# One block from the projection on, an early second feed product, and turnings moved in the output product

## The reference, cut to what matters

```python
n = _rms_norm(x, norm_attn_g)
q, k, v of both mixers = n @ w_in                      # 3072 columns
mixed = concat(diff_attention(...), stick_breaking(...))  # 512 + 512 columns
h = x + mixed @ w_out
n2 = _rms_norm(h, norm_ffn_g)
y = h + (silu(n2 @ w_gate) * (n2 @ w_up)) @ w_down      # D_FF = 2816
y = _rms_norm(y, norm_final_g)
```

## Time and profile before

| What | Value |
|---|---|
| median of 3 runs | 1412.73 us (1412.57 to 1413.26) |
| the profiled execution, its own time | 1409.75 us |
| its span in the profile | 1407.9 us |
| busy, PE | 1361.4 us, 97% of the span |
| busy, DVE | 999.7 us, 71% |
| busy, ACT | 623.8 us, 44% |
| busy, POOL | 450.8 us, 32% |
| mean granted clock | 0.993 |

### The profile page before, as it was taken

The page is one execution under the profiler, slowest core; times in us unless marked ns, Lnnn a source line. Parts: engine busy times, 40 slices in busy tenths (PEclk is TensorE's granted clock), DMA queues, the critical chain, the costliest instruction groups (busy, mean ns, idle before and its releaser), DMA issues. The chain is left out here.

```text
span 1407.9 us, 23796 instructions
## 1 busy us (share of the span) xinstructions
PE 1361.4 (97%) x9152; PEld 1193.8 (85%) x9152; DVE 999.7 (71%) x1317; ACT 623.8 (44%) x1112; POOL 450.8 (32%) x416
## 2 busy tenths in 40 slices
PE   6999999989999999999789999999999999999997
PEld 5778888768888777788689999999999998787886
DVE  5896858688868999756687766566766566754466
ACT  6634333288887887333352122222132233533343
POOL 2133341200010000111174454454454454644353
PEclk9999999999999999999999999999999999999999
DMA  7265542464444544433234543444443448855554
GB/s 254 72 213 192 204 154 73 146 181 138 126 127 121 148 136 135 156 127 96 65 121 144 174 137 123 150 145 145 174 143 116 150 163 290 303 175 164 164 180 172
DMA packets 172200, 218.05 MB, mean 155 GB/s; under 512 B 19836, under 2 KB 110328, under 8 KB 170680
## 3 DMA queue, kind: packets, MB, share of 16 engines
q1 hardware_dynamic: 163416, 193.13, 42.3%
q0 software_dynamic: 3840, 12.58, 2.7%
q10 hardware_dynamic: 4832, 10.82, 2.1%
HBM read 152.98 MB, written 63.50 MB: 154 GB/s over the span
## 5 line engine op out<-in xcount | busy, mean ns | idle before, releaser
L792 PE MATMUL ps_proj<-shared 128*128 128x512 f32 x224 | 90.1, 402 | 2.7 <-DVE shared L546 1.8
L2663 ACT COPY aux<-ps_feed 128x544 f32<-128x544 f32 x22 | 13.5, 612 | 170.3 <-PE ps_feed L2984 170.3
L793 PE MATMUL ps_proj<-shared 128*128 128x512 f32 x224 | 88.1, 393 | 0.0
L794 PE MATMUL ps_proj<-shared 128*128 128x512 f32 x224 | 88.1, 393 | 0.0
L2613 POOL TENSOR_TENSOR ring_more<-staging,ring_more 128x512 fp32r<-128x512 f32 x45 | 69.5, 1550 | 56.5 <-ACT ring_more L2649 56.4
L2613 POOL TENSOR_TENSOR shared<-staging,shared 128x512 fp32r<-128x512 f32 x41 | 60.0, 1467 | 86.1 <-ACT shared L2649 86.1
L1431 ACT COPY aT<-ps_aT 128x512 f32<-128x512 f32 (+2 forms) x168 | 81.1, 526 | 9.8 <-PE ps_aT L1760 9.0
L1760 PE MATMUL ps_aT<-ident,z 128*128 128x128 f32 (+1 forms) x568 | 83.3, 280 | 1.9 <-DVE z L1603 1.7
L2877 DVE TENSOR_TENSOR blocks<-ps_feed,blocks 128x512 f32<-128x512 f32 x56 | 36.0, 682 | 66.4 <-PE ps_feed L3013 66.4
L1603 DVE TENSOR_TENSOR_SCAN z<-z,near 128x1024 f32<-128x1024 f32 (+7 forms) x64 | 81.5, 1336 | 0.0
L2982 PE MATMUL ps_feed<-shared,ring_more 128*128 128x272 f32 x264 | 76.6, 290 | 2.4 <-issue 2.4
(11 more groups left out here) (372 smaller groups left out, 4520.5 us busy)
## 6 DMA issues: line engine op xcount, KB each, us to landing
staging<-s_dram SPq DMA_DIRECT2D x50, 256.0 KB, 4.2
staging<-in_w_gate SPq DMA_DIRECT2D x11, 1024.0 KB, 7.8
blocks<-in_w_up SPq DMA_DIRECT2D x11, 1024.0 KB, 5.3
blocks<-in_w_down SPq DMA_DIRECT2D x11, 1024.0 KB, 9.8
t_dram<-blocks SPq DMA_DIRECT2D x11, 1024.0 KB, 3.9
s_dram<-blocks SPq DMA_DIRECT2D x11, 1024.0 KB, 5.2
w_raw<-in_w_in SPq DMA_DIRECT2D x10, 1024.0 KB, 6.6
staging<-in_cache_sb_v POOLq DMA_DIRECT2D x31, 256.0 KB, 3.1
```

Source lines behind the costliest of these rows:

```text
L792: nc.tensor.matmul(res, a_hi[:, k, cols], b_hi[:, k], start=start, stop=False)
L793: nc.tensor.matmul(res, a_hi[:, k, cols], b_lo[:, k], start=False, stop=False)
L794: return nc.tensor.matmul(res, a_lo[:, k, cols], b_hi[:, k], start=False, stop=(k == HK - 1))
L2663: nc.scalar.copy(two(first), bank(u, 0)).then_inc(first_done, 1)
```

## The change

It has four parts.

1. **One block.** `feed` uses `t["block"]`, and `border.close()` comes after it, so no engine waits at the end of mix.
2. **Product 1 of unit 0 early.** `early_product_pe` makes product 0 and then product 1 behind tile 8's matmuls, ahead of `turn_n(8)`; the second waits for the sums of tile 7. Weight block 1 is split into mT_lo in place of `shared`, by ACT right behind block 0 and by POOL right behind block 0; POOL now first waits for the normed rows of tile 7. Feed's PE loop starts at product 2.
3. **Left columns of product 2 (the third) without the sample.** For c = 0 it waits for `n_lo` of the first three chunks only. ACT splits weight block 2 ahead of the last columns of part 2, and waits for two products ahead of the split of part 6.
4. **Turnings.** `turn_m(1)` goes ahead of the last 24 matmuls of tile 0, and `turn_m(2)` behind the left half of tile 1, ahead of `turn_n(0)`.

```diff
 mix:
-        t["ring_first"][0] = [mT_hi[:, late, a * HK:(a + 1) * HK] for a in range(2)]
+        t["ring_first"] = [[x[:, late, a * HK:(a + 1) * HK] for a in range(2)] for x in (mT_hi, mT_lo)]
...
@ gpsimd
-                if i >= NT - 1:
-                    w_low_pool(nc, pool, t, i - NT + 1)
+                if i == NT - 1:
+                    pool.wait_ge(normed, NT - 1)
+                    w_low_pool(nc, pool, t, 0)
+                    w_low_pool(nc, pool, t, 1)
...
@ scalar
-                if i == NT:
-
-                    act.wait_ge(mixed, 2 * NT)
-                    w_high_act(nc, act, t, 1)
...
                         w_high_act(nc, act, t, 0)
+                        w_high_act(nc, act, t, 1)
...
@ tensor
             turn_m(0)
             multiply_first(1, range(HK, KD))
+            turn_m(1)
             pe.wait_ge(m_lo, 2)
             multiply_first(0, range(HK)).then_inc(mixed, 1)
-            turn_m(1)
             multiply_first(1, range(HK)).then_inc(mixed, 1)
             pe.wait_ge(*t["outputs_made"])
             for i in range(1, NT):
-                if i + 1 < NT:
+                if 2 < i + 1 < NT:
                     turn_m(i + 1)
...
+                    if j == 0 and i == 1:
+                        turn_m(2)
                     if j == 0:
                         turn_n(i - 1)
             pe.wait_ge(m_lo, 2 * NT)
-            first_product_pe(nc, pe, t, 3 * NC - 2)
+            early_product_pe(nc, pe, t, 0, 3 * NC - 2)
+            pe.wait_ge(h_added, 2 * (NT - 1))
+            early_product_pe(nc, pe, t, 1, 3 * NC - 1)
             turn_n(NT - 1)
...
 early_product_pe(nc, pe, t, m, parts_done), in place of first_product_pe:
-    pe.wait_ge(t["w_lo_done"], 1)
+    pe.wait_ge(t["w_lo_done"], m + 1)
     pe.wait_ge(t["n_lo"], parts_done)
-    w_hi, w_lo = t["ring_first"][0]
+    w_hi, w_lo = t["ring_first"][m]
-        res = t["ps"][:, 0, c, 0:CW]
+        res = t["ps"][:, m, c, 0:CW]
-            x_hi, x_lo = t["part_hi"][0][:, k, cols], t["part_lo"][0][:, k, cols]
+            x_hi, x_lo = t["part_hi"][m][:, k, cols], t["part_lo"][m][:, k, cols]
...
 feed:
-        block = ctx.enter_context(nc.Block(no_gpsimd_drain=True))
+        block = t["block"]
...
@ scalar
+            split_w(2)
             split_n(2)
-            split_w(2)
             split_n(3)
             split_w(3)
...
                 if u == 0 and s in (0, 1, 2):
+                    if s == 2:
+                        act.wait_ge(multiplied, 2)
                     split_n(4 + s)
...
@ tensor
-                if u == 0:
-                    pe.wait_ge(n_lo, parts_done(s))
                 pe.wait_ge(w_lo_done, m + 1)
                 w_hi, w_lo = ring[m % RING]
                 for c in range(2):
+                    if u == 0 and s == 2 and c == 0:
+                        pe.wait_ge(n_lo, 3 * (NT // 2 - 1))
+                    elif u == 0:
+                        pe.wait_ge(n_lo, parts_done(s))
...
-                for s in range(0 if u else 1, NPROD):
+                for s in range(0 if u else 2, NPROD):
                     product(u, s)
...
 encoder_step:
             mix(nc, t)
-            border.close()
             feed(nc, t)
+            border.close()
```

More of the change, by code:

```diff
@@ L2225, in w_low_pool, with early_product_pe @@
     nc.gpsimd.tensor_tensor(w_lo, first_blocks(t)[m], w_hi.bitcast(F32), ALU.subtract).then_inc(t["w_lo_done"], 1)
-def first_product_pe(nc, pe, t, parts_done):
-    pe.wait_ge(t["w_lo_done"], 1)
+def early_product_pe(nc, pe, t, m, parts_done):
+    pe.wait_ge(t["w_lo_done"], m + 1)
     pe.wait_ge(t["n_lo"], parts_done)
-    w_hi, w_lo = t["ring_first"][0]
+    w_hi, w_lo = t["ring_first"][m]
     HK, CW = w_hi.shape[1], t["half"] // 2
@@ L3163, in encoder_step @@
                                 .rearrange("p (k n) -> p k n", k=HK) for a in range(2))
-            at = 6 * WIDTH + 2 * HK * P
-            t["ring_first"] = [None, [shared[:, at + a * HK * P:at + (a + 1) * HK * P]
-                                      .rearrange("p (k n) -> p k n", k=HK) for a in range(2)]]
             mix(nc, t)
+            feed(nc, t)
             border.close()
-            feed(nc, t)
 _INS = ['x_prompt', 'x_sample', 'cache_diff_k', 'cache_diff_v', 'cache_sb_k', 'cache_sb_v', 'norm_attn_g', 'w_in',
```

## The result

The changed kernel took 1414.88 us, median of 22 runs (1412.96 to 1417.08), against 1412.74 us for the kernel before over 22 runs beside it (1410.71 to 1415.44). The ratio is 1.0018, with a 95% interval of 1.0012 to 1.0023: some 2.5 us slower (2.1 us by the medians), clear of zero, and by the bound of 0.2% still no change that a single measurement could tell. The profiled execution took 1416.36 us (span 1414.4 us), one of the longer ones.

A forecast was written before the change was run, and what follows sets the result against it. PE was taken to bound the start, DVE's chain the seam. Terms +1.5 + 0.05 + 0.16 = +1.7 us gave 1411.4 us for the profiled execution, 1414.4 us for the median; range 1410.6 to 1418.2 us.

The forecast's parts named there:

- The hole behind turning 2: Start of output product: PE waits 4.2 us for tile 0's normalised rows, whose turning starts 1.5 us later.
- Turning 1 costs nothing: Turning 1, ahead of tile 0's last 24 matmuls, finds its input ready; costed at nothing, some tenths if that cover went.
- Tile 7's normalisation: At the seam, L2039 runs without POOL's collision, so tile 7's row turning on PE gains 1.02 us.
- Two POOL instructions delay DVE by 2 x 1.2 us: POOL's two weight-split instructions move onto five DVE additions behind tile 7's normalisation and delay them, 2.4 us in all.
- First early product: PE's first early product, waiting for DVE's first L2047, starts at 690.2 instead of 689.52 us.
- Turning 8 and the block's end: At the seam, turning 8 with ACT's copies comes +0.05 us later; the long split that starts DVE's chain, +0.16 us.
- the encounter of POOL with L2732: POOL's L2613 (1.3 us) meets the DVE step the prediction calls L2731, which ends at 701.75 instead of 701.10 us.
- Products 2 and 3 early: At the seam, 4.4 us leave PE and the third product finishes some 3 us sooner; neither is waited for, no gain.
- the bound at the seam: DVE's chain, not PE, sets the seam; the rival that PE sets it had chance 0.07 and gave 1408.8 us.
- The clock: Rival, chance 0.38: granted clock falls in the new hole behind turning 2, costing 3 us, 1417.4 us.
- main case: Start and seam terms summed, no added clock fall: 1414.4 us, own range 1412.0 to 1415.5 us, chance 0.45.

The follow-up runs named there:

- x6: c with tile 0's square, normalisation and additions moved ahead of work waiting on turning 2 or tile 2's heads, turnings kept; 1407.94 us, ratio 0.9976 to the kernel before.
- x2: c with 16 added matmuls of 512 columns, read by nothing, in PE's hole behind turning 2; 1412.33 us, ratio 1.0001 to the kernel before.
- c: The changed kernel itself, with all four parts of the change; 1414.88 us, ratio 1.0018 to the kernel before.
- x1: c with turning 2 back at the head of tile 1's product, turning 1 still early; 1412.62 us, ratio 1.0003 to the kernel before.
- x3: c without POOL's wait for tile 7's normalised rows; 1415.72 us, ratio 1.0022 to the kernel before.
- x8: The kernel before with one block in place of two and nothing else; 1412.67 us, ratio 1.0003 to the kernel before.
- x4: c with the second early product behind the last turning instead of ahead of it; 1415.43 us, ratio 1.0023 to the kernel before.
- x12: c with the third product waiting for all its columns ahead of the left ones; 1415.75 us, ratio 1.0023 to the kernel before.
- x9: x6 with DVE's two weight sums moved out from ahead of the first two parts' low halves; 1407.98 us, ratio 0.9972 to the kernel before.
- x10: x6 with ACT's split of weight block 2 back behind the last columns of part 2; 1408.19 us, ratio 0.9968 to the kernel before.
- x5: c with both turnings where they stood before, leaving only the seam's change; 1413.41 us, ratio 1.0009 to the kernel before.

## Why the prediction was right, point by point

The forecast was 1414.4 us, slower by less than can be told; measured were 1414.88 us.

- **The hole behind turning 2, +1.5 us.** Right, in place and size: 22.37 - 20.97 = +1.40 us, with a wait of 3.96 us on the normalisation (worked out: 4.2 us). x6 shows the cause, x2 that PE's own work has no part in it. "Turning 1 costs nothing" held: it stands at 6.14 us in place of 8.95 us and nothing waited for it. One thing I had missed did no harm: wherever turning 1 is early, tile 2's heads wait for their load (DVE idle 2.5 to 3.1 us ahead of L903, 3.11 us in c), so sooner turnings alone would have brought turning 2's input no sooner; in x1 turning 2 kept its 14.89 us.
- **Tile 7's normalisation, -1.02 us on PE.** Right: turning 7 less tile 0's turning went from 87.35 us to 86.39 us in x2.
- **Two POOL instructions delay DVE by 2 x 1.2 us.** Right in kind, 2 x 1.1 us in size (1.78 - 0.68). First early product: +0.7 us worked out; 117.74 - 112.94 less the 4.1 us that came from the start is +0.7 us. x3 shows that the wait ahead of it is worth nothing.
- **Turning 8 and the block's end, +0.05 and +0.16 us.** The seventh product came 0.1 us sooner instead of 0.2 us later. x8 measured the block's end at 0.38 us (0.40 us in the sum); the encounter of POOL with L2732 came as described, 0.96 us long.
- **Products 2 and 3 early, nothing.** Right; x4 starts the second 5.0 us and the third 2.7 us later for 0.35 us, x12 the third 1.7 us later for 0.0 us. In x9 and x10 PE's work stays and the chain through ACT and DVE shrinks, and the seventh product comes sooner by what the long split does: 0.78 and 0.44 us at the split, 0.77 and 0.40 us at the product. So the bound at the seam is shown.
- **The clock, a rival at 0.38 and 3 us.** Here the weights were off, not the mechanism. In all four profiles with the 4.2 us hole (c, x3, x4, x12) the clock fell there, and it cost 2.7 us. By itself this would have made 1.4 + 2.7 - 0.1 = 4 us, outside the main case. It didn't, because the kernel before pays a smaller fine of the same kind: its hole of 2.5 us, which x1, x5 and x8 keep, was followed by a fall in these three of four profiles, for 1.3 to 1.5 us. That the executions of the kernel before without a profile mostly have it too is inferred; its one profile, without the fall, lies 2.98 us below the median, which fits. I had taken from the one profile of before that such a hole does no harm. An estimate from these counts: 4.0 - 0.75 x 1.4 = 3.0 us, against 2.5 us measured. So the sum was closer than its reasoning deserved: it left out two terms of opposite sign, of which +2.7 us is the larger and the one that the rival named.

Eight profiles are few to say how often each hole makes the clock fall; that stays open.

## What to carry to other kernels

When an instruction is moved later in one queue, list what stands behind it in the queues that consume its result: here ACT's square and DVE's normalisation, which had nothing to do with the turning, were held by it, and PE met them again one instruction later. Where the matrix engine idles at a seam, moving its work forward buys nothing as long as another engine's chain ends last; shorten that chain, and look for its collisions with POOL. A hole in a dense stretch costs its length and then the low clock behind it, so an order with no hole at all can win by more than the hole's length: tile 0's turning is 4.2 us nearer in x6 than in x1 (18.26 against 22.42 us), whose hole was 2.55 us long. By the times x6 beat the kernel before by 3.4 us, with an interval of 1.7 to 5.1 us.

## What was unexpected of the hardware

- A hole of 2.5 us in otherwise dense matmuls was followed by half the granted clock in three of four profiles, for a shorter time (x1 at 0.50 from 592 to 595 us) than behind the hole of 4.2 us (0.51 from 600.4 to 607.2 us). The Trainium skill (TensorE: Matmul & The Clock Gate, "What's actually happening") names two states, throttled and full. The traces agree: no stretch showed another level that a mixture of the two doesn't give.
- POOL and DVE held each other up even at POOL's one-column instruction: L68 took 0.70 us beside a DVE addition of two SBUF tensors (x9), 0.18 us with DVE idle (x10). A DVE addition with one operand in PSUM was not held up: c's L2788 took 0.71 us within a POOL instruction of 1.29 us, and the 22 executions of that line took 0.706 to 0.725 us each.
- Useless matmuls can shorten a program: 16 of them, 4.0 us of PE's time in x2, took 2.7 us out of the path.
